# Turning the operands of a small product around: the 16 columns of dt as the stationary side, in the first block of a two-block layer

## What is computed

```python
hn = rms_norm(h, norm_mix_g[l])
proj = jnp.einsum('bsd,de->bse', hn, w_in[l])
za, zb, zc, xbc, dt_raw, g_raw = jnp.split(proj, SPLIT_POINTS, axis=-1)
...
dt = jax.nn.softplus((dt_raw + dt_bias).astype(jnp.float32))
a = -jnp.exp(a_log.astype(jnp.float32))
xdt = x32 * dt.reshape(bsz, nc, q, g, r)[..., None]
adt = (dt * a).reshape(bsz, nc, q, g, r).transpose(0, 3, 4, 1, 2)
a_cs = jnp.cumsum(adt, axis=-1)
```

## Time and profile before

| | us |
|---|---|
| median of 3 runs | 1411.72 |
| lowest, highest | 1407.47, 1413.49 |
| the profiled execution, its own time | 1413.53 |
| its span in the trace | 1411.7 |
| PE busy in the span | 1265.0 (90%) |
| DVE, ACT, POOL busy | 830.7, 590.8, 842.1 |
| mean granted PE clock | 0.945 |

### The profile page before, as it was taken

How to read it: one execution, slowest core, us unless ns; L and a number is a source line. 1 busy time by engine, 2 the same in 40 slices (tenths; PEclk the granted TensorE clock), 3 DMA queues, 4 the chain that set the end, 5 groups by cost and what they waited for, 6 DMA issues and landing times. The chain is left out here.

```text
span 1411.7 us, 26925 instructions
## 1 busy us (share of the span) xinstructions
PE 1265.0 (90%) x11640; PEld 1182.6 (84%) x11640; DVE 830.7 (59%) x1113; ACT 590.8 (42%) x899; POOL 842.1 (60%) x348
## 2 busy tenths in 40 slices
PE   6998899879588899998899999996559998999997
PEld 6998789869588799997899998995449997899996
DVE  2396837592759434444566666185887644555565
ACT  5337444528243444445444445442331101644443
POOL 5757354665568498885598884982020003598884
PEclk9999999989799999999999999997668999999999
DMA  6544134344246365554365655551000002465652
GB/s 241 189 128 149 58 120 125 114 150 135 79 145 210 122 191 182 191 182 148 107 192 182 192 182 180 187 166 59 15 0 4 5 4 78 138 188 184 189 183 86
DMA packets 53254, 189.79 MB, mean 134 GB/s; under 512 B 6160, under 2 KB 7312, under 8 KB 53008
## 3 DMA queue, kind: packets, MB, share of 16 engines
q1 hardware_dynamic: 50256, 181.95, 40.3%
q10 hardware_dynamic: 2880, 6.12, 1.2%
HBM read 187.00 MB, written 1.05 MB: 133 GB/s over the span
## 5 line engine op out<-in xcount | busy, mean ns | idle before, releaser
L471 POOL TENSOR_TENSOR weight_lo<-raw_ring,weight_hi 128x1024 fp32r<-128x1024 f32 x342 | 831.9, 2450 | 469.4 <-ACT weight_hi L1988 456.5
L1988 ACT ACTIVATE weight_hi<-raw_ring 128x1024 fp32r<-128x1024 f32 x338 | 355.4, 1058 | 453.5 <-DMA raw_ring<-in_ffn_gu 113.5
L493 PE MATMUL product<-operand_B_hi,weight_hi 128*128 128x256 f32 x1104 | 314.0, 284 | 22.9 <-DVE arena L1186 18.8
L495 PE MATMUL product<-operand_B_hi,weight_lo 128*128 128x256 f32 x1104 | 312.5, 283 | 0.0
L494 PE MATMUL product<-operand_B_lo,weight_hi 128*128 128x256 f32 x1104 | 312.3, 283 | 0.0
L493 PE MATMUL product<-operand_A_hi,weight_hi 128*128 128x256 f32 x840 | 242.9, 289 | 26.5 <-DVE weight_lo L1209 11.4
L494 PE MATMUL product<-operand_A_lo,weight_hi 128*128 128x256 f32 x840 | 240.5, 286 | 0.0
L495 PE MATMUL product<-operand_A_hi,weight_lo 128*128 128x256 f32 x840 | 240.4, 286 | 0.0
L493 PEld LDWEIGHTS product<-operand_B_hi,weight_hi 128*128 128x128 f32 x1104 | 209.9, 190 | 26.6 <-issue 22.1
L494 PEld LDWEIGHTS product<-operand_B_lo,weight_hi 128*128 128x128 f32 x1104 | 209.8, 190 | 3.1
L495 PEld LDWEIGHTS product<-operand_B_hi,weight_lo 128*128 128x128 f32 x1104 | 209.5, 190 | 0.0
(11 more groups left out here) (336 smaller groups left out, 1717.3 us busy)
## 6 DMA issues: line engine op xcount, KB each, us to landing
raw_ring<-in_w_in SPq DMA_DIRECT2D x107, 512.0 KB, 3.5
raw_ring<-in_ffn_gu SPq DMA_DIRECT2D x88, 512.0 KB, 3.7
raw_ring<-in_ffn_down SPq DMA_DIRECT2D x44, 512.0 KB, 3.7
raw_ring<-in_w_mlp_up SPq DMA_DIRECT2D x32, 512.0 KB, 3.5
raw_ring<-in_w_mlp_down SPq DMA_DIRECT2D x32, 512.0 KB, 3.5
raw_ring<-in_w_out SPq DMA_DIRECT2D x16, 512.0 KB, 3.4
raw_ring<-in_w_branch_c SPq DMA_DIRECT2D x8, 512.0 KB, 3.5
raw_ring<-in_w_branch_a SPq DMA_DIRECT2D x8, 512.0 KB, 3.4
```

The source lines that it names most:

```text
L471: k.nc.gpsimd.tensor_tensor(k.wlo[:, slot, 0:w], k.raw[:, slot, 0:w], k.whi[:, slot, 0:w].bitcast(F32), ALU.subtract).then_inc(k.s["lo_rea ...
L493: mm(ps, w_hi, op.hi[:, b, :], start=b == 0, stop=False)
L495: return mm(ps, w_lo, op.hi[:, b, :], start=False, stop=b == blocks - 1)
L1988: k.nc.scalar.activation(k.whi[:, slot, 0:w], k.raw[:, slot, 0:w], ACT.Copy).then_inc(k.s["hi_ready"], 1)
```

## The change

The products for dt swap sides. `W_dt` (128 inputs x 16 columns) becomes the stationary operand and the activations (128 inputs x 256 tokens) move, so that both halves of the tokens go in one matmul: 24 matmuls with an output of 16 partitions x 256 tokens in `bank[1]`, in the place of 48 with an output of 128x16. The matmuls that turned the row factors go. DVE multiplies the 16x256 sums by the row factors, ahead of the evacuations of v0 to v3, and writes them to `dt_rows` (the space of `rv`, which is not in use until later). PE transposes them to tokens, two 128x16 outputs in `bank[2]`, behind v4, the fifth tile of v. Behind v7's evacuation DVE then only adds the bias; the copy of the factors goes.

```diff
@@ allocate
     k.rv = sb("rv", [P, T])
+    k.dt_rows = k.rv
@@ tensor_program
     pe.wait_ge(s["late_in"], 128)
-    for ch in range(NCH):
-        last = mm(k.bank[1][:, ch:ch + 1], k.rs[:, ch * P:(ch + 1) * P], k.ident[:, 0:1], start=True, stop=True)
+    op, ps = k.made["hn"], k.bank[1][0:16, 0:T]
+    for b in range(KB):
+        mm(ps, k.wdt_hi[:, b, :], op.hi[:, b, :], start=b == 0, stop=False)
+        mm(ps, k.wdt_hi[:, b, :], op.lo[:, b, :], start=False, stop=False)
+        last = mm(ps, k.wdt_lo[:, b, :], op.hi[:, b, :], start=False, stop=b == KB - 1)
     last.then_inc(s["dt_mm"], 1)
-    op = k.made["hn"]
-    for ch in range(NCH):
-        tok = slice(ch * P, (ch + 1) * P)
-        for b in range(KB):
-            ps = k.bank[2][:, ch * 16:ch * 16 + 16]
-            mm(ps, op.hi[:, b, tok], k.wdt_hi[:, b, :], start=b == 0, stop=False)
-            mm(ps, op.lo[:, b, tok], k.wdt_hi[:, b, :], start=False, stop=False)
-            last = mm(ps, op.hi[:, b, tok], k.wdt_lo[:, b, :], start=False, stop=b == KB - 1)
-    last.then_inc(s["dt_mm"], 1)
-    dense(k, pe, "v")
+
+    def dt_by_token(i):
+        if i == 4:
+            pe.wait_ge(s["dt_scaled"], 1)
+            for ch in range(NCH):
+                last = k.nc.tensor.transpose(k.bank[2][:, ch * 16:ch * 16 + 16], k.dt_rows[0:16, ch * P:(ch + 1) * P],
+                                             k.ident[0:16, 0:16])
+            last.then_inc(s["dt_mm"], 1)
+
+    dense(k, pe, "v", after=dt_by_token)
     dense(k, pe, "u")
@@ vector_program
     ssd_conv(2)
+    v.wait_ge(s["dt_mm"], 1)
+    nv.tensor_tensor(k.dt_rows[0:16, :], k.bank[1][0:16, 0:T], k.rs[0:16, :], ALU.mult).then_inc(s["dt_scaled"], 1)
     vector_to_scalar(k, v, "v", 0, 4)
     ssd_conv(3)
     vector_to_scalar(k, v, "v", 4, 8)
-    v.wait_ge(s["dt_mm"], 1)
-    st.do(nv.tensor_copy(c.rs_col, k.bank[1][:, 0:2]))
     v.wait_ge(s["dt_mm"], 2)
-    st.settle()
     for ch in range(NCH):
-        st.do(nv.scalar_tensor_tensor(c.z[:, ch * 16:ch * 16 + 16], k.bank[2][:, ch * 16:ch * 16 + 16],
-                                      c.rs_col[:, ch:ch + 1], c.dtb, ALU.mult, ALU.add))
+        st.do(nv.tensor_tensor(c.z[:, ch * 16:ch * 16 + 16], k.bank[2][:, ch * 16:ch * 16 + 16], c.dtb, ALU.add))
```

2 lines of the change are left out of this document (1 added, 1 removed).

## The result

The kernel after took 1419.99 us (median of 11 runs, 1417.23 to 1424.45), the kernel before 1414.54 us beside it (11 runs, 1407.47 to 1418.74): a ratio of 1.0043, with a 95% interval of 1.0024 to 1.0061. Three further series gave 1.0023 [0.9992, 1.0053], 1.0015 [0.9989, 1.004] and 1.0034 [1.0004, 1.0063]. One run of the first of these, at 2440.31 us, is in none of the figures here. So the kernel after is slower by 0.15 to 0.43%, about 4 us on average. I had predicted 1409.5 us and a gain of 2.2; the time lies outside my range of 1405.5 to 1414.0. Of the 10.5 us between forecast and measurement 2.8 are the base: I had subtracted from 1411.72, the median of three runs of before, and with eight more it is 1414.54.

A forecast was written before the change was run, and what follows sets the result against it. DVE was taken to bound from 89.7 to 122.3 us, then PE and DVE's dt chain waiting for POOL. The chain's 2.4 us less 0.2 allowance gave 1411.72 - 2.2 = 1409.5 us, range 1405.5 to 1414.0.

The forecast's parts named there:

- The products for dt: On PE ahead of v0: 24 products at 0.119 us, 2.9 us in place of 7.5, ending at 89.5; worth nothing there.
- DVE's sum: On DVE around v0 to v3: scaling adds 0.33 us, the 0.30 us pause for v3 goes; net none.
- The evacuations of v4 to v7 stay at 122.3.: On DVE behind the fourth convolution: these evacuations start at 122.3 us as before, since the convolution hides PE's savings.
- the chain for dt: Small DVE instructions behind u3: starting 1.2 us sooner, they wait one POOL instruction less, moving u4's evacuation 2.4 us to 144.8.
- My slower rival: PE runs v4 to v7 too long at half clock behind its pause; up to 2.6 us later, 1414.3 us; chance 0.07.
- v4 to v7, u0 and u1: On PE: 3.9 us pause ahead of v4, 1.0 us lost to clock; u0 at full clock, u1 waits for POOL, 1.2 us sooner.
- my first rival: No gain reaches the end: u0 still at half clock, or dt's chain misses its earlier POOL slot; 1411.7 us; no-gain chance 0.30.
- whole instructions: At DVE's chain for dt: shared ports are held per instruction, so the shift is 0 or 2.4 us, never 1.2.
- my rival "smooth": At DVE's chain for dt: POOL's instructions move with the rest, so the gain is PE's 1.2 us, 1410.5 us; chance 0.10.
- What is late next: ACT's line behind u4's evacuation moves 2.4 us, so L1308 (`xdec`) starts at 151.1; 2.2 us gained after 0.2 allowance.
- The sum: Whole kernel: the 2.2 us gained at 153.43 (0 to 2.4) is carried to the end, giving 1409.5 us; chance 0.50.

The follow-up runs named there:

- e_scale_late: Kernel after, but DVE scales dt behind the fourth convolution and PE transposes behind v7 in place of behind v4; ratio 1.0005 to before.
- e_late_again: e_scale_late once more, unchanged, in a later session; ratio 1.0001 to before, median 1414.96 us.
- e_two_scalings: Kernel after with DVE's scaling of dt done twice, once more into rows that nobody reads; ratio 1.0 to before.
- b_again: Kernel before, unchanged, profiled and timed a second time; ratio 0.9993 to before.
- b_third: Kernel before, unchanged, profiled and timed a third time; ratio 0.999 to before.
- a_again: Kernel after, unchanged, profiled and timed once more; ratio 1.0023 to before.
- b_few kernels: Kernel before with 16 in place of 48 dt products, three of the four with one added DVE instruction of different widths; 0.9993, 1.0009, 1.0016, 1.0005.
- e_high_late: e_scale_late, with ACT also making the first high part of each half of v ahead of the SiLU; ratio 1.0018 to before.
- e_filler: Kernel after with the 48 old dt products added behind the 24 new ones, into a bank nobody reads; ratio 1.0009 to before.

## Why the prediction was wrong

**The products for dt: right.** 24 products at 0.114 us from start to start, the last at 87.59, no half clock behind them and v0 to v3 at full clock. The estimate of 0.119 us was a little high. The two transposes took 0.29 us, where I had 0.5.

**DVE's sum: right as a sum, wrong as an argument.** The scaling took 0.34 us (104.11 to 104.45; I had 0.33), and DVE's wait for v3 went. I wrote "+0.33 - 0.30, none", and took it that nothing moves when the sum is zero. But the two sit at different places. The evacuations of v0 to v3 and the start of the convolution are now a fixed train behind the end of the third convolution, as is POOL's request through ACT (SiLU, high part). In before, DVE's wait for PE loosened the two against each other: POOL's request came at +0.24, +0.28 us and, where v3 was late, ahead of the convolution. In after it came at +0.36 in all four profiles, and starved each time.

**The first failed step: "The evacuations of v4 to v7 stay at 122.3."** It rested on POOL's low parts staying where they were, and I never asked whether the low part of v5's weights would still take 2.4 us. I had read POOL's rows as times at which its instructions start, and had weighed that DVE waits for POOL, in the chain for dt. The reverse, that POOL waits for DVE, isn't in the prediction at all. It costs PE 4.33 us ahead of v5 and a half clock of 6.86 us behind it, and DVE comes to v7 at 125.45 where the earlier trace rows had 122.30 for v4 to v7 together. The prediction named this test ("DVE's evacuations of v4 to v7 at 122.3"), and it fails there. By lengths it holds in e_scale_late and e_late_again, where POOL is served in turns: 31.3 us behind the third convolution's first instruction, as in before. My slower rival had the right sign and another cause, a PE at half clock from v4 to v7; a low part that takes longer stood in none of the rivals.

**v4 to v7, u0 and u1.** The pause ahead of v4 and its fall of the clock came as said, and e_scale_late shows them harmless. u0 at full clock and u1's wait for POOL couldn't be seen in after, where PE is held up by v5. Both came in e_scale_late (0.54 us at 124.99). In e_late_again, the same kernel, u0 ran at half clock, as my first rival had it. So this step was right in one launch of two.

**The second failed step, the chain for dt: "it waits one POOL instruction less, and the whole chain moves by one of these, 2.4 us".** This was the whole of the gain that I forecast. In e_scale_late the chain began 1.6 us sooner and met a POOL instruction one place earlier, but its end moved by 0.7 us: L1281 (L1279 in before), which had taken 0.20 us, waited for POOL's last low part. The earlier trace rows had shown me that POOL had just stopped at 146.05, so a chain 2.4 us sooner must meet it still running, and I moved the chain without asking that. The end of the chain hangs on when POOL's last low part ends, and neither "whole instructions" nor my rival "smooth" describes it. In after the evacuation of u4 is at 144.88, which looks like my 144.8. It is no hit: the third convolution had started 1.63 us sooner in that launch (89.39 against 91.02), so 0.65 us of the 2.28 are the change's. I had forecast clock times, and only a length can be compared between launches. The 2.0 us of e_two_scalings are no hit either, since they come from a shorter convolution.

**"What is late next": incomplete.** I followed ACT's line to `xdec` and compared nothing of POOL there, though the earlier trace rows had shown what one contest costs. It was lost in all six profiles in which v5's low part was starved.

**The rule that I leaned on.** `xdec` behind a POOL instruction took 2.97 us in place of 1.40; a low part of 2.4 us behind DVE's convolution took 7.96 us, beside 15 instructions of under half a microsecond. The Trainium skill, page "SBUF — State Buffer", section "SBUF: two separate sides", says that whoever starts first keeps the shared ports for the whole instruction and that the other is blocked. For DVE behind POOL the trace agrees, with the 2.97 us. For POOL behind DVE that is not all: POOL was blocked not by one instruction but by all that stood in DVE's queue.

**The total.** The sum was to be -2.2 us. Up to 187 us it came out at +1.3 us in M (the mean of the six starved profiles, 96.8, against 95.5), so 3.5 us are missing there. Of these, 2.2 are the gain, of which nothing is left in X (62.3 on average in the six and in before); of it 1.6 to 2.0 us were never there, since the kernels with nothing starved gain only 0.2 to 0.6, and the rest is the event's. The other 1.3 us are the mean of the 0.8 to 1.9 at `xdec`. The times say +4.0 us (the mean of the four series of after). The other 2.7 us arise behind 187 us, where I had written that a difference of more than 3 us "would be something that I have not seen"; no run here shows their cause.

**What stays open.** Behind 187 us one profile of the kernel before differs from another by 2.3 us, and the kernels here spread over 18 us. One place of many is PE's wait for an operand at 455 us. The waits of PE from 445 to 470 us in before, and then in after:

```profile
PE bank L550 <- DVE operand_A_lo L1155: 4.8, 1, 4.8
```

```profile
PE bank L551 <- DVE operand_A_lo L1159: 8.1, 1, 8.1
```

The two look different, but b_again had 2.2 us there, b_third 7.6 and a_again 7.5. Taken as means of times less M, the kernels with the change lose some 2 us behind 187 us, starved or not, and the b_few kernels 0.4. With errors of 0.6 to 0.8 on each that is a hint and no proof, and no run tells which part of the change would do it. e_high_late, with the shortest M and a time 2.8 us above before, belongs to it.

## What to carry to other kernels

When two engines share a resource, an edit whose sum is zero still moves one engine's train of instructions against the other's, and the question is who stands behind whom at the next contest; ask for it in both directions, also for the engine with room to spare. If PE needs the next tile's weights, make them before a run of back-to-back DVE instructions and not beside it: with the high part made one place earlier X was 1.1 to 2.2 us shorter, because what then had to wait was a low part that PE needed later. A chain that waits for another engine at each step ends when that engine's last piece ends; starting the chain sooner gains little. Compare lengths between two landmarks and not clock times, and don't promise that a gain in one stretch reaches the end: here the three kernels that gained 2 us in the stretch were no faster in the total, and no version beat the kernel before by more than the error.

## What the runs showed of the hardware

A waiting GpSimd instruction can be passed over by a whole run of VectorE instructions: 7.96 us in place of 2.4, beside instructions that follow each other every 0.32 to 0.40 us. Where the two take turns, each switch costs VectorE 2.1 us (2.48 us in place of 0.40), so that the same convolution takes 6.1 us undisturbed and lasts 14.8 us, up to the next evacuation, in turns.

For the low part of v5's weights, repeated profiles of a kernel with the change agreed in this each time. With the change it came at +0.29 us (twice, 8.02 and 8.04 us) and +0.36 us (four times, 7.95 and 7.96 us), and not at -0.28, -0.07 and +0.63; in the kernel before and its variants not at +0.24, +0.27, +0.28, +0.33 and +0.40. That the two sets overlap is the part for which I have no explanation. Later in the same convolution low parts were starved at +2.1, +2.4 (twice, once in a variant of the kernel before) and +7.4 us, for 6.0 to 7.2 us.

Products with a stationary side of 16 columns and 256 columns moving went at 0.114 us from start to start, against 0.119 for 128 stationary columns, and the clock stayed at its upper level behind 24 of them. In before it fell at 90.38, in the run of products with 16 columns moving, though PE never paused there. In e_filler, where the 48 old products follow the 24 new ones, it fell at 92.8 for 3.4 us, about where the old ones end.
